# A single-core transformer kernel: first transfers reordered, four projection groups split over the contraction, bias rows fetched at the third partial sum

## What is computed

```python
c_act = jax.nn.silu(c)                                   # c: (1, 1024)
mod = c_act @ w_ada[l] + b_ada[l]                        # w_ada: (1024, 6*1024)
sh1, sc1, ga1, sh2, sc2, ga2 = jnp.split(mod, 6, axis=-1)
u = modulate(rmsnorm(h, g_norm1[l]), sh1, sc1)           # h: (1, 256, 1024)
y = hybrid_mixer(u, w_in[l], ...)                        # first step: proj = u @ w_in
h = h + ga1[:, None, :] * y
u2 = modulate(rmsnorm(h, g_norm2[l]), sh2, sc2)
y2 = hierarchical_moe(u2, ...)                           # 32 experts
h = h + ga2[:, None, :] * y2
modf = c_act @ w_ada_f + b_ada_f                         # (1024, 2*1024)
```

## Time and profile before

| | before |
|---|---|
| median of 3 runs | 2326.28 us (2326.18 to 2326.29) |
| the profiled execution's own time | 2326.34 us |
| its span in the profile | 2324.6 us |
| PE busy | 2272.2 us (98%) |
| DVE busy | 1169.1 us (50%) |
| ACT busy | 428.5 us (18%) |
| DMA | 499.82 MB, mean 215 GB/s |

### The profile page before, as it was taken

One profiled execution on the slowest core, in us unless ns is written; L12 is line 12 of the kernel. 1 busy time (PEld: TensorE's weight loads), 2 busy tenths in 40 slices (PEclk: granted clock), 3 DMA queues, 4 the chain that ended last, 5 costly groups with the idle time before them and its releaser, 6 DMA issues.

```text
span 2324.6 us, 30016 instructions
## 1 busy us (share of the span) xinstructions
PE 2272.2 (98%) x12500; PEld 1551.9 (67%) x12500; DVE 1169.1 (50%) x2169; ACT 428.5 (18%) x858; POOL 51.0 (2%) x77
## 2 busy tenths in 40 slices
PE   6999999999999989999999999999999999999998
PEld 4778855444444458849877768847866977676873
DVE  2788431111111166668663356666676665235665
ACT  1123321111111011101323211102101231221110
POOL 1000100000000010000000000000000000000000
PEclk9999999999999999999999999999999999999999
DMA  9656578999999974435330545527445342144541
GB/s 397 257 217 250 229 210 340 422 422 422 422 422 422 421 228 153 179 131 187 119 137 2 181 135 165 179 93 233 166 163 181 128 163 92 42 141 154 181 165 53
DMA packets 176003, 499.82 MB, mean 215 GB/s; under 512 B 6904, under 2 KB 99336, under 8 KB 146064
## 3 DMA queue, kind: packets, MB, share of 16 engines
q1 hardware_dynamic: 171920, 481.23, 55.0%
q0 software_dynamic: 3824, 16.43, 2.3%
q10 hardware_dynamic: 144, 0.52, 0.1%
HBM read 491.34 MB, written 6.82 MB: 214 GB/s over the span
## 4 chain that ended last, share of the span: by engine, by line
PE 89%; DMA 8%; DVE 1%; ACT 1%; issue 0%; SPq 0%; POOL 0%; DVEq 0%; POOLq 0%
PE bank L2193 21%; PE bank L2233 11%; PE bank L1435 7%; DMA ring<-in_w 7%; PE bank L871 6%; PE bank L2297 6%; PE bank L1472 3%; PE bank L2545 3%; PE bank L2407 2%; PE bank L2678 2%; PE bank L2171 2%; PE bank L2724 2%; PE bank L1419 2%; PE bank L2401 2%; PE bank L2648 2%; PE bank L1456 2%
## 5 line engine op out<-in xcount | busy, mean ns | idle before, releaser
L2193 PE MATMUL bank<-Tw,Sx 128*128 128x256 f32 x960 | 213.8, 379 | 0.0
L2193 PEld LDWEIGHTS bank<-Tw,Sx 128*128 128x128 f32 x960 | 179.3, 190 | 22.7
L871 PE MATMUL bank<-xT,ring 128*128 128x256 f32 x640 | 143.6, 384 | 2.8 <-ACT xT L283 2.8
L2193 PE MATMUL bank<-ring,xT 128*128 128x256 f32 x640 | 144.7, 379 | 0.0
L871 PEld LDWEIGHTS bank<-xT,ring 128*128 128x128 f32 x640 | 122.7, 193 | 21.8 <-ACT xT L283 2.9
L2193 PEld LDWEIGHTS bank<-ring,xT 128*128 128x128 f32 x640 | 121.6, 190 | 18.2 <-issue 1.9
L1435 PE MATMUL bank<-ring,xg 128*64 128x512 f32 x512 | 113.9, 593 | 5.4 <-DMA ring<-in_w 5.4
L1472 PE MATMUL bank<-ring,hTg 128*64 128x512 f32 x512 | 113.4, 595 | 0.0
L1770 DVE TENSOR_TENSOR sg<-sg,bank 128x512 f32<-128x512 f32 x16 | 11.0, 687 | 203.0 <-PE bank L1435 203.0
L1435 PE MATMUL bank<-more,xg 128*64 128x512 f32 x512 | 112.6, 592 | 0.0
L2233 PE MATMUL bank<-Tw,Sx 128*128 128x512 f32 x240 | 108.9, 592 | 0.0
(11 more groups left out here) (571 smaller groups left out, 3795.4 us busy)
## 6 DMA issues: line engine op xcount, KB each, us to landing
ring<-in_w SPq DMA_DIRECT2D x128, 1024.0 KB, 17.7
ring<-in_ffn_w_in SPq DMA_DIRECT2D x88, 1024.0 KB, 7.6
ring<-in_first_pieces SPq DMA_DIRECT2D x33, 2048.0 KB, 12.5
more<-in_w SPq DMA_DIRECT2D x64, 1024.0 KB, 17.5
ring<-in_ffn_w_out SPq DMA_DIRECT2D x20, 2048.0 KB, 7.8
ring<-in_w_mix_in SPq DMA_DIRECT2D x12, 2048.0 KB, 7.7
ring<-in_xattn_w_kv SPq DMA_DIRECT2D x8, 2048.0 KB, 8.1
ring<-in_w_mix_out SPq DMA_DIRECT2D x4, 2048.0 KB, 9.6
```

The lines of the kernel that those rows point to most:

```text
L871: last = nc.tensor.matmul(b[:, c * SEQ:(c + 1) * SEQ], w[:, k, m * P:(m + 1) * P], xT[:, k, :], start=(k == 0), stop=(k == KD - 1))
L2193: last = nc.tensor.matmul(bank[BANK_OF[name]][:, 0:SEQ], lhs(k), rhs(k), start=(k == 0), stop=(k == 3))
```

## The change

The first two "in" pieces are cut along the contraction instead of the columns. Piece ("head", 0) holds rows 0 to 511 of the first 1024 columns of `w_in`, ("head", 1) rows 512 to 1023. The list now begins with ada 0, ada 2, head 0, ada 1, ada 3, head 1; behind them the ada piece comes ahead of the in piece in each pair, and the two last ada pieces stand alone. Shift and scale are made in two halves, first for blocks 0 to 3 (from ada 0 and 2), then for 4 to 7. Blocks 4 to 7 are copied from PSUM without modulation (their banks are needed) and modulated in place. Groups 0 to 3 begin with half of the contraction (`head(g, 0)`), between the partial sums, and end with the other half. The second load of constants is issued with the ninth piece instead of the fifth. GpSimd fetches the bias rows at the third partial sum, not at the end of group 0, and the router's weights behind them. The products of ada 4 to 8 stand after groups 3, 5, 7, 10, 12 instead of 1, 3, 5, 7, 10, and VectorE's sums and taps are ordered anew up to the first level. In the second network the semaphore `mx_x` is replaced by `xs_dve`, with the same waits.

```diff
-PIECES1 = ([("ada", n) for n in range(4)] + [p for n in range(12) for p in (("in", n), ("ada", n + 4))]
+ADA_FIRST = (0, 2, 1, 3)
+PIECES1 = ([("ada", 0), ("ada", 2), ("head", 0), ("ada", 1), ("ada", 3), ("head", 1)]
+           + [p for n in range(10) for p in (("ada", n + 4), ("in", n + 2))] + [("ada", 14), ("ada", 15)]
...
                 if kind == "ada" and n < 4:
-                    sp.wait_ge(ada_part, n + 1)
+                    sp.wait_ge(ada_part, ADA_FIRST.index(n) + 1)
+                elif kind == "head":
+                    if n == 0:
+                        sp.wait_ge(head_half, 1)
+                    else:
+                        sp.wait_ge(proj_full, 4)
...
-                if j == SLOTS:
+                if j == 2 * SLOTS:
                     sp.dma_start(K[:, NCONST_FIRST:, :], a["const_tiles"][:, NCONST_FIRST:, :]
...
-            pool.wait_ge(proj_full, 1)
+            pool.wait_ge(ada_part, 3)
...
+            head(0, 0)
+            head(1, 0)
             ada_partial(2)
-            ada_columns(1)
+            head(2, 0, (0,))
             ada_partial(3)
+            head(2, 0, (1,))
             ada_columns(2)
             ada_columns(3)
-            pe.wait_ge(xT_act, 1)
-            pe.wait_ge(xT_dve, 1)
+            head(3, 0).then_inc(head_half, 1)
+            pe.wait_ge(xT_act, 2)
+            pe.wait_ge(xT_dve, 2)
...
-            for i, g in enumerate((1, 3, 5, 7, 10)):
+            for i, g in enumerate((3, 5, 7, 10, 12)):
                 after[g].append(("ada", 4 + i))
...
             dve.wait_ge(proj_dve, 2)
-            ada_sum(6)
-            convolve(6)
-            ada_sum(7)
...
+            convolve(3)
+            ada_sum(5)
+            convolve(1)
+            ada_take(5)
+            ada_sum(6)
+            keys(0)
+            convolve(2)
+            ada_sum(7)
+            keys(1)
+            ada_take(6)
...
-            ada_take(8)
-            convolve(3)
+            ada_take(7)
+            convolve(6)
...
+            ada_sum(8)
             dve.wait_ge(consts_loaded, 48)
...
-                if l > 1:
-                    ada_take(7 + l)
+                ada_take(7 + l)
```

More of the change, by code:

```diff
@@ L793, in tensor1, with ada_partial, ada_columns @@
             pe.wait_ge(consts_loaded, 32)
-            def ada_partial(i):
-                s = wait_piece(pe, J1["ada", i])
+            def ada_partial(p):
+                s = wait_piece(pe, J1["ada", ADA_FIRST[p]])
                 w = slot_w(s, KD, 512)
-                if i >= 2:
-                    pe.wait_ge(ada_copied, i - 1)
+                if p >= 2:
+                    pe.wait_ge(ada_copied, p - 1)
                 for k in range(KD):
                     q = slice((k % 4) * 32, (k % 4) * 32 + 32)
-                    last = nc.tensor.matmul(bank[6 + i % 2][q, :], c_act[:, k:k + 1].to_broadcast([P, 32]), w[:, k, :],
+                    last = nc.tensor.matmul(bank[6 + p % 2][q, :], c_act[:, k:k + 1].to_broadcast([P, 32]), w[:, k, :],
                                             start=(k < 4), stop=(k >= 4))
                 last.then_inc(ada_part, 1)
-            def ada_columns(i):
-                pe.wait_ge(ada_copied, i + 1)
+            def ada_columns(p):
+                pe.wait_ge(ada_copied, p + 1)
+                at = 4 * ADA_FIRST[p]
                 for c in range(4):
-                    last = nc.tensor.matmul(bank[5][:, 4 * i + c:4 * i + c + 1], acc[:, i % 2, c * P:(c + 1) * P],
+                    last = nc.tensor.matmul(bank[5][:, at + c:at + c + 1], acc[:, p % 2, c * P:(c + 1) * P],
                                             one_each[:, 0:1], start=True, stop=True)
@@ L832, in tensor1 @@
             norm_transposes(pe, 0, 0)
+            ada_columns(0)
             ada_partial(1)
-            ada_columns(0)
+            ada_columns(1)
+            pe.wait_ge(xT_act, 1)
+            pe.wait_ge(xT_dve, 1)
+            def head(g, part, cs=(0, 1)):
+                w = slot_w(wait_piece(pe, J1["head", part]), 4, 1024)
+                for c in cs:
+                    for k in range(4):
+                        last = nc.tensor.matmul(bank[g][:, c * SEQ:(c + 1) * SEQ],
+                                                w[:, k, g * 256 + c * P:g * 256 + (c + 1) * P], xT[:, 4 * part + k, :],
+                                                start=((part, c, k) == (0, 0, 0)), stop=((part, c, k) == (1, 1, 3)))
+                return last
+            head(0, 0)
+            head(1, 0)
             ada_partial(2)
-            ada_columns(1)
+            head(2, 0, (0,))
             ada_partial(3)
+            head(2, 0, (1,))
             ada_columns(2)
             ada_columns(3)
-            pe.wait_ge(xT_act, 1)
-            pe.wait_ge(xT_dve, 1)
+            head(3, 0).then_inc(head_half, 1)
+            pe.wait_ge(xT_act, 2)
+            pe.wait_ge(xT_dve, 2)
             def project(g):
@@ L846, in project @@
                 b = bank[g % NB]
-                if g == G_A1:
+                if g < NB:
+                    last = head(g, 1)
+                elif g == G_A1:
                     pe.wait_ge(rows_loaded, ROWS)
@@ L1011, in scalar1, with ada_copy @@
             norm_sums(act, 0)
[L1012 to L1016, removed]
-            act.wait_ge(mod_ready, 1)
-            xT_by_act(act, 0, mcol[:, 1, :], mcol[:, 0, :])
+            def ada_copy(p):
+                act.wait_ge(ada_part, p + 1)
+                if p >= 2:
+                    act.wait_ge(ada_psum, p - 1)
+                nc.scalar.activation(acc[:, p % 2, :], bank[6 + p % 2][:, :], ACT.Copy).then_inc(ada_copied, 1)
+            ada_copy(0)
+            for k in (4, 5):
+                act.wait_ge(tr_full, k // 2 + 1)
+                st(nc.scalar.activation(xT[:, k, :], tr_bank(k), ACT.Copy))
+            ada_copy(1)
+            act.wait_ge(mod_ready, 1)
+            for k in (0, 1):
+                act.wait_ge(tr_full, k // 2 + 1)
+                last = nc.scalar.activation(xT[:, k, :], tr_bank(k), ACT.Identity, scale=mcol[:, 1, k:k + 1],
+                                            bias=mcol[:, 0, k:k + 1])
+            last.then_inc(xT_act, 1)
+            ada_copy(2)
+            ada_copy(3)
+            act.wait_ge(mod_ready, 2)
+            st.sync()
+            for k in (4, 5):
+                last = nc.scalar.activation(xT[:, k, :], xT[:, k, :], ACT.Identity, scale=mcol[:, 1, k:k + 1],
+                                            bias=mcol[:, 0, k:k + 1])
+            last.then_inc(xT_act, 1)
             def full(g):
@@ L1150, in ada_take, with modulation @@
                     nc.vector.tensor_tensor(r, bank[5][:, :], r, ALU.add).then_inc(ada_taken, 1)
[L1152 to L1157, removed]
+            def modulation(n, i, ks, shift, scale, gain):
+                st(nc.vector.tensor_tensor(mcol[:, i, ks], mcol[:, i, ks], column(cols, C1, shift)[:, ks], ALU.add))
+                st(nc.vector.scalar_tensor_tensor(out=mcol[:, i + 1, ks], in0=mcol[:, i + 1, ks], scalar=1.0,
+                                                  in1=column(cols, C1, scale)[:, ks], op0=ALU.add, op1=ALU.add))
                 st.sync()
-                nc.vector.tensor_tensor(mcol[:, i + 1, :], mcol[:, i + 1, :], column(cols, C1, gain),
+                nc.vector.tensor_tensor(mcol[:, i + 1, ks], mcol[:, i + 1, ks], column(cols, C1, gain)[:, ks],
                                         ALU.mult).then_inc(mod_ready, 1)
@@ L1166, in vector1 @@
             dve.wait_ge(c_ready, 1)
[L1167 to L1170, removed]
+            for k in (6, 7):
+                dve.wait_ge(tr_full, k // 2 + 1)
+                st(nc.vector.tensor_copy(xT[:, k, :], tr_bank(k)))
+            for half in range(2):
+                ada_take(2 * half + 1)
+                dve.wait_ge(ada_taken, half + 1)
+                modulation(half, 0, slice(4 * half, 4 * half + 4), "sh1", "sc1", "g_norm1")
+                for k in (4 * half + 2, 4 * half + 3):
+                    src = xT[:, k, :] if half else tr_bank(k)
+                    last = nc.vector.tensor_scalar(xT[:, k, :], src, mcol[:, 1, k:k + 1], mcol[:, 0, k:k + 1],
+                                                   ALU.mult, ALU.add)
+                last.then_inc(xT_dve, 1)
             wd = column(cols, C1, "w_dw").rearrange("p (k n) -> p k n", k=4)
@@ L1361, in vector1 @@
             dve.wait_ge(ada_taken, ADA_ROWS)
-            modulation(1, "sh2", "sc2", "g_norm2")
+            modulation(2, 2, slice(0, KD), "sh2", "sc2", "g_norm2")
             xT_by_dve(dve, 3, mcol[:, 3, :], mcol[:, 2, :])
@@ L1381, in tensor_moe @@
             values(1, range(1))
-            pe.wait_ge(xT_act, 3)
-            pe.wait_ge(xT_dve, 2)
+            pe.wait_ge(xT_act, 4)
+            pe.wait_ge(xT_dve, 3)
             for t in range(NT):
@@ L3658 @@
         pieces["ada", n] = rows_of(i["w_ada"][0][:, n * 512:(n + 1) * 512])
-        pieces["in", n] = rows_of(w_in[:, PROJ_COLS[n]:PROJ_COLS[n] + 512])
```

(3 more changed lines are left out.)

48 lines of the change are left out of this document (22 added, 26 removed).

## The result

| | before | changed |
|---|---|---|
| median | 2326.28 us (5 runs) | 2336.36 us (2335.04 to 2339.37, 5 runs) |
| ratio | | 1.0044, 95% interval 1.0032 to 1.0057 |
| span of the profiled execution | 2324.6 us | 2334.6 us |

The changed kernel is slower by 10.1 us, 0.44%. 2335.4 us had been forecast, in a range of 2328 to 2342.

The account below looks back on a forecast made before the run. TensorE was taken to set the pace, with VectorE and the DMA queue close behind. A 7.6 us delay at the second attention product plus 1.5 for the clock gave 9.1 on 2326.34: 2335.4 us, range 2328 to 2342.

Parts of the forecast that it names:

- The start: Up to group 4: first half-contraction at about 24.1, group 4 at 60.4 instead of 67.19, a lead of 5.9 us.
- The term for the lowered clock: Behind the wait before the first projection matmul: 2.0 us charged for the lower clock, ends 1.5 and 2.8.
- To level 1: Group 4 to level 1: TensorE waits 2 us around piece 8's sum; level 1 at 127.9 against 132.23, lead 4.3.
- The loop: Levels 2 to 7: "ada 10" to "ada 14" requested a level later; lead 2.3 at level 2, 5.9 behind at level 7.
- The last step: After level 7: "ada 15" summed by 246.0, last row addition ends at 254.7, second attention product 7.6 us late.
- The clock: New waits before levels 4 and 6 and the last rows: one clock fall of 1.5 us taken, ends 0 and 7.2.
- The bias rows: 2 MB requested near 36 find the sixth piece nearly landed: costed at nothing, up to 2 us if it is late.

Follow-up runs that it names:

- run 5: Changed kernel with GpSimd fetching the bias rows at the end of group 0 again, not at the third partial sum: 2349.64 us, ratio 1.0104 to before.
- run 1: Changed kernel with each in piece again ahead of its ada piece from 'ada 7' on: 2322.12 us, ratio 0.9987 to before.
- run 3: Changed kernel with the old piece order from 'ada 7' on and the sum of 8 ahead of the decay values: 2320.30 us, ratio 0.9977.
- run 4: Kernel before with 'ada 10' to 'ada 14' one place later in the list, nothing else: 2332.62 us, ratio 1.0036.
- run 2: Changed kernel with VectorE's order alone edited, the sum of piece 8 ahead of the decay values as before: 2337.36 us, ratio 1.0044 to before.

## Why the prediction was right, step by step

- **The start** was forecast with a lead of 5.9 us at group 4 (60.4). It was 4.0 (62.30, and the one product less). The first matmul was at 24.56, not 24.1. The term for the lowered clock was too small: 2.0 charged, 9.94 instead of 6.91 measured, so 3.0, just over its end of 2.8. How much it is differs between executions of the same code: 7.15 in run 5, 8.56 and 8.60 in runs 1 and 3. "ada 4" landed 7.8 us after its request, as priced.
- **To level 1**: a lead of 4.3 forecast, 0.9 found. TensorE waited 2.18 for the sum of 8, as forecast (2); the rest is the start, and a group at the lowered clock behind that wait (8.72 instead of 7.03, both from the timeline), which I had counted for no place ahead of level 4.
- **The loop** went by the mechanism named: the second of a pair landed 12.3 to 13.3 us after its issue (12.4), 12.7 to 13.7 after its release (12.9), and the sums of 10 to 14 waited. Level 4 started at 188.6 (forecast 185.5), level 6 at 227.0 (223.4), level 7 at 247.65 (241.6). So at level 7 the delay was 11.9 us, twice the 5.9 of the forecast: 3.6 was there at level 6, about what the lead at level 1 had fallen short (3.4), and 2.5 came between levels 6 and 7, where the forecast had no wait. The sum of 14 waited 7.43 us for its piece, the longest wait of all, and TensorE behind it 0.32 for the sum and 1.59 for the layer norm's product. TensorE's waits for the scaled pair stood before levels 3 and 5, not 4 and 6. Runs 1 and 4 show the cause from both sides. That the start and the place of the sum matter less is shown by runs 2 and 3.
- **The last step** was wrong: "ada 15" did not hold the second attention product. Its sum ran at 243.30 without waiting, and the delay at the pointwise product is that at level 7, 11.9 us. The forecast put 1.7 us of its 7.6 there.
- **The clock** was the mis-sized term. One fall of 1.5 us was taken. There were three new ones behind the start, read from the timelines: 1.7 (8.72 at 122.56 against 7.03 for such a group), 1.8 (8.86 at 141.87 against 7.07) and 1.6 (level 3: 3.68 against 2.05 at level 5). Their sum of 5.1 is within the stated end of 7.2. None of them stood before levels 4 or 6, the places I named, and the one at 141.87 had no wait of TensorE close ahead of it. By the rule that I took from the Trainium skill, "TensorE: Matmul & The Clock Gate", section "HAM oscillation — how this bites in real kernels", every recurring wait would have been followed by a fall; of TensorE's four waits of about 2 us those at 24.56, 120.55 and 170.07 were, that of 199.42 was not, and in run 5 that of 23.92 was not either. The Trainium skill's case there has waits longer than the work between them, and here they are shorter, so I had stretched the rule.
- **The bias rows** were costed at nothing, and that holds; the reason, that the sixth piece had nearly landed, is what the trace shows. What the early fetch saves, 13.3 us in this order and with one count for all of GpSimd's transfers, the prediction did not see.

The mechanism was the one named, but the total of 9.1 us against 10.1 measured is in good part luck. Where the forecast had 7.6 and 1.5, the waits and the clock came to 11.9 at the pointwise product, which starts at 263.27 and not at 259; a wait in the last step was forecast that did not come, and 1.9 of the 11.9 did not reach the end.

## What to carry to other kernels

When transfers to one queue wait for their slots in order, the event that frees a slot times not only its own transfer but all behind it. After a reordering write down for each transfer which event lets go the one ahead of it, and how late its own consumer may be. An earlier start is kept only if the next engine's work and its transfers are moved forward with it. And a semaphore that counts several transfers holds its first user until the last of them has landed.

## What the runs showed that was not expected

- Two queues share the engines unevenly: from 50 to 60 us in run 5 GpSimd's queue moved 17% of the bytes (0.69 of 4.03 MB), and an 18 KB transfer at its end landed 24.1 us after its issue, against 7.0 in a free stretch.
- A pause in the main queue is worth something: 2 MB of rows passed in it, and moving them out of it cost 13.3 us, through an addition that waited for all seven transfers of a common count.
- The same start of the kernel, behind the same wait of 1.80 us, took 7.15 us for its first 16 projection matmuls in run 5 (clock 1.00), 8.56 and 8.60 in runs 1 and 3, and 9.94 in the changed kernel and run 2.
- In the second network, where the change replaces one semaphore and nothing else, a difference of 12.9 us shrank to 10.0 in two steps, at two stretches where the clock was lower in the other execution.
